# A hybrid GLA and dilated-attention layer on eight cores: x loaded as bf16 through the GpSimd DMA queue, and the transposes of the GLA output moved to the merge

## The reference, cut to what matters

```python
h = x @ w_in
gq, gk, gv, gg, g_lr, dq, dk, dv, gate_a, gate_b = jnp.split(h, SPLIT_AT, axis=-1)
logd = jax.nn.log_sigmoid((g_lr @ w_gk_b + b_gk).astype(jnp.float32)) / GLA_NORMALIZER
o, S = gla_recurrence(...)
o = o * lax.rsqrt(jnp.mean(jnp.square(o), -1, keepdims=True) + NORM_EPS) * gla_norm
o = o * jax.nn.silu(gg.reshape(B, T, GLA_HEADS, GLA_DV).astype(jnp.float32))
ya = o.reshape(B, T, GLA_V).astype(x.dtype) @ w_br_gla
...
m = jax.nn.sigmoid(gate_a) * ya + jax.nn.sigmoid(gate_b) * yb
x = layer_norm(ALPHA * x + m @ w_out, ln1_g, ln1_b)
```

## Time and profile before

| | us |
|---|---|
| median of 2 runs | 5650.87 (5649.4 to 5652.34) |
| the profiled execution, its own time | 5676.41 |
| span of that execution, slowest core | 5675.1 |
| spans of the 8 cores | 5634.0 to 5675.1 |
| mean granted clock of PE, share of full speed | 0.738 to 0.743 |

### The profile page before, as it was taken

How to read it: one execution, slowest core, us unless ns; L and a number is a source line. 1 busy time by engine, 2 the same in 40 slices (tenths; PEclk the granted TensorE clock), 3 DMA queues, 4 the chain that set the end, 5 groups by cost and what they waited for, 6 DMA issues and landing times.

```text
span 5675.1 us, 71363 instructions; the slowest of 8 cores (5634.0 to 5675.1 us)
## 1 busy us (share of the span) xinstructions
PE 3560.3 (63%) x23137; PEld 2106.4 (37%) x23326; DVE 2144.8 (38%) x4185; ACT 1498.2 (26%) x3227; POOL 561.9 (10%) x666
## 2 busy tenths in 40 slices
PE   0346777778658658658658658658658656344454
PEld 0123334335335435335435335435435424233333
DVE  1111223344444444435435435435435434322223
ACT  0112222224224224224224224224224213111111
POOL 0000111110100100100100100100100111100011
PEclk9667788886876876876876876876876877755556
DMA  9998444442532532532532532532532555576774
GB/s 130 147 151 164 132 139 146 153 147 72 170 110 73 180 114 72 177 111 80 175 113 80 171 117 80 170 118 83 174 114 87 165 179 180 188 154 134 141 173 151
DMA packets 219423, 768.24 MB, mean 135 GB/s; under 512 B 19788, under 2 KB 41102, under 8 KB 216600
## 3 DMA queue, kind: packets, MB, share of 16 engines
q0 software_dynamic: 166176, 650.26, 43.1%
q1 hardware_dynamic: 52888, 113.41, 6.1%
HBM read 832.46 MB, written 75.91 MB: 160 GB/s over the span
## 4 chain that ended last, share of the span: by engine, by line
PE 52%; DVE 17%; DMA 13%; issue 7%; ACT 7%; another core or an unknown queue 2%; DVEq 1%; ACTq 0%; SPq 0%; POOLq 0%
PE pr L230 42%; DMA sb_wb<-scr_w_in 6%; PE pl L230 5%; PE pr L234 3%; DVE sb_g_xres L252 2%; PE pb L234 2%; DVE sb_g_cacc L261 1%; DVE sb_Sst L261 1%; DVE sb_stats L692 1%; DMA sb_g_xres<-xh 1%; ACT sb_aext L241 1%; ACT sb_kTc L241 1%; DVE sb_rA L252 1%; DMA sb_wb<-scr_w_out 1%
## 5 line engine op out<-in xcount | busy, mean ns | idle before, releaser
L230 PE MATMUL pr<-sb_wb,sb_g_xT 128*128 128x512 bf16 x4028 | 1099.3, 430 | 158.2 <-DMA sb_wb<-scr_w_in 133.4
L230 PE MATMUL pr<-sb_g_xT,sb_wb 128*128 128x256 bf16 (+3 forms) x4008 | 493.2, 282 | 400.9 <-DMA sb_wb<-scr_w_in 168.4
L230 PEld LDWEIGHTS pr<-sb_wb,sb_g_xT 128*128 128x128 bf16 x4184 | 451.4, 110 | 755.5 <-issue 410.6
L139 POOL DMA_DIRECT2D sb_wb<-scr_w_in x318 | 281.7, 887 | 2960.1 <-PE pr L230 2828.6
L230 PEld LDWEIGHTS pr<-sb_g_xT,sb_wb 128*128 128x128 bf16 (+1 forms) x4008 | 381.3, 102 | 509.6 <-issue 453.1
L249 ACT ACTIVATE sb_PT<-pr 128x512 bf16<-128x512 f32 x816 | 483.1, 597 | 214.7 <-PE pr L230 207.0
L234 PE MATMUL pr<-sb_idf,sb_g_xres 128*128 128x128 f32 x784 | 152.4, 357 | 590.4 <-DVE sb_g_xres L252 253.7
L230 PE MATMUL pr<-sb_g_qT,sb_kTr 64*128 64x128 bf16 x3264 | 464.9, 295 | 0.0
L234 PEld LDWEIGHTS pr<-sb_idf,sb_g_xres 128*128 128x128 f32 x784 | 122.8, 186 | 617.8 <-issue 616.9
L230 PE MATMUL pl<-sb_Vr,sb_PT 128*128 128x65 bf16 x3264 | 321.5, 239 | 36.5 <-DVE sb_PT L252 28.4
L230 PEld LDWEIGHTS pr<-sb_g_qT,sb_kTr 64*128 64x128 bf16 x3264 | 263.9, 124 | 73.2 <-issue 2.8
(11 more groups left out here) (229 smaller groups left out, 4434.8 us busy)
## 6 DMA issues: line engine op xcount, KB each, us to landing
sb_wb<-scr_w_in POOLq DMA_DIRECT2D x284, 1024.0 KB, 7.3
sb_wb<-scr_w_up POOLq DMA_DIRECT2D x100, 1024.0 KB, 8.2
sb_wb<-scr_w_down POOLq DMA_DIRECT2D x40, 1024.0 KB, 8.1
sb_g_xres<-xh SPq DMA_DIRECT2D x64, 512.0 KB, 5.7
sb_kvc<-kvc POOLq DMA_DIRECT2D x16, 2048.0 KB, 13.0
sb_lnp<-lnp SPq DMA_DIRECT2D x60, 512.0 KB, 4.0
sb_wb<-scr_w_brg POOLq DMA_DIRECT2D x20, 1024.0 KB, 7.5
sb_wb<-scr_w_out POOLq DMA_DIRECT2D x20, 1024.0 KB, 8.1
```

The lines of the kernel that those rows point to most:

```text
L139: ins = q.h.dma_start(out=out, in_=in_, **kw)
L230: fw.op(pe, lambda: nc.tensor.matmul(out, lhsT, rhs, start=start, stop=stop), reads=reads, writes=writes, skip_self=True)
```

## The change

It has two parts and a small one.

1. **x as bf16, loaded by POOL.** A new buffer `xbf` (two tiles, bf16) is filled by `issue_xb` through POOL's queue, which converts on the way. The first group's load is issued before the loop; the load for the next group is issued right after the transposes of the present one and ahead of the weight loads of `gla_prep`. The transposes read `xbf` by `transpose_b16`: eight blocks into the one bank `pb` and one copy of 1024 columns per tile, instead of two buffers and two copies of 512. The float32 load of x by SP is kept only in full groups, for the residual.
2. **The transposes of the GLA output later.** `onb` becomes a buffer per tile of the group (`onb[:, j, ...]`), and the transposes leave `gla_out_norm` for a function of their own, `gla_out_T(j)`, which `merge_out` calls for all tiles before its first projection.
3. `cvo`, the staging tile of the convolution state, becomes a name for `rA`. The `K_PAD` lines do nothing unless a variable is set.

```diff
-        onb = T("onb", (128, 1024), BF16)
...
-        cvo = T("cvo", (32, 512))
+        cvo = rA
...
+        xbf = Tp("xbf", (128, G, D), BF16)
...
-                stt(onb[:, h * 256:(h + 1) * 256], PL[h // 2][:, (h % 2) * 256:(h % 2 + 1) * 256], ssq[:, 4 + h:5 + h],
+                stt(onb[:, j, h * 256:(h + 1) * 256], PL[h // 2][:, (h % 2) * 256:(h % 2 + 1) * 256], ssq[:, 4 + h:5 + h],
...
-            transpose_b16(lambda c: onb[:, c * 128:(c + 1) * 128], 8,
-                          lambda c0, n_: onT[:, c0:c0 + n_, j * 128:(j + 1) * 128], [R("onb")], [R("onT", j)])
+
+        def gla_out_T(j):
+            transpose_b16(lambda c: onb[:, j, c * 128:(c + 1) * 128], 8,
+                          lambda c0, n_: onT[:, c0:c0 + n_, j * 128:(j + 1) * 128], [R("onb", j)], [R("onT", j)])
...
         def merge_out(tiles):
             n = len(tiles)
             ln_load(0)
+            for j in range(n):
+                gla_out_T(j)
...
-        _issued = False
+
+        def issue_xb(tiles_):
+            for j_, t_ in enumerate(tiles_):
+                fw.dma(pool, xbf[:, j_, :], xsrc(t_), writes=[R("xbf", j_)])
+
+        issue_xb(_glist[0][0])
...
-            load_x(tiles, xsrc, ridx if kind != "state" else None, issued=_issued)
-            _issued = False
-            if kind != "full" and _gi + 1 < len(_glist):
-                _nt, _nk = _glist[_gi + 1]
-                issue_x(_nt, xsrc, ridx if _nk != "state" else None)
-                _issued = True
+            if kind == "full":
+                for j, t in enumerate(tiles):
+                    fw.dma(sp, xres[:, j, :], xsrc(t), writes=[R("xres", j)])
+            if kind != "state":
+                for j, t in enumerate(tiles):
+                    fw.dma(sp, ropet[j][:], rope_d[ridx(t)], writes=[R("ropet", j)])
+            for j, t in enumerate(tiles):
+                transpose_b16(lambda c, j=j: xbf[:, j, c * 128:(c + 1) * 128], 8,
+                              lambda c0, n_, j=j: xT[:, c0:c0 + n_, j * 128:(j + 1) * 128], [R("xbf", j)], [R("xT", j)])
+            if _gi + 1 < len(_glist):
+                issue_xb(_glist[_gi + 1][0])
```

More of the change, by code:

```diff
@@ L345, in alloc_group_bufs @@
             d["ggn"] = TT("ggn", (128, g_, 1024), BF16)
-            d["onT"] = TT("onT", (128, 8, n_), BF16)
+            d["onT"] = TT("onT", (128, 8, n_), BF16); d["onb"] = TT("onb", (128, g_, 1024), BF16)
             d["qT"] = [TT(f"qT{g}", (128, g_, 4, 128), BF16) for g in range(3)]
@@ L356, in _build @@
         Ebl = _gb["Ebl"]; eblT = _gb["eblT"]; qtT = _gb["qtT"]; ktT = _gb["ktT"]; khat = _gb["khat"]; vb = _gb["vb"]
-        ggn = _gb["ggn"]; onT = _gb["onT"]; qT = _gb["qT"]; attnT = _gb["attnT"]; mb = _gb["mb"]; mT = _gb["mT"]
+        ggn = _gb["ggn"]; onT = _gb["onT"]; onb = _gb["onb"]; qT = _gb["qT"]; attnT = _gb["attnT"]; mb = _gb["mb"]; mT = _gb["mT"]
         cacc = _gb["cacc"]; gl = _gb["gl"]; yT = _gb["yT"]; pT = _gb["pT"]
@@ L361, in _build @@
         Sst = Tp("Sst", (128, NH, DV)); Sbf = Tp("Sbf", (128, NH, DV), BF16)
+        xbf = Tp("xbf", (128, G, D), BF16)
         aext = [Tp(f"aext{i}", (128, 2 + NMAX)) for i in range(2)]
         tails = Tp("tails", (128, NFC, 2))
+        _pad = int(os.environ.get("K_PAD", "0"))
+        if _pad:
+            padbuf = Tp("padbuf", (128, _pad))
         RS = [NDEL[g] + G - 1 for g in range(3)]
@@ L882, in _build @@
                 tp(ps[0:2, c * 128:(c + 1) * 128], tails[:, fc, :], idf[:], [R("tails"), RC], [rp])
-            evac(cvo[0:2, 0:nf * 128], ps[0:2, 0:nf * 128], [rp], [R("cvo")], eng=dve)
-            fw.dma(sp, cv_p[:, f4 * 512:f4 * 512 + nf * 128], cvo[0:2, 0:nf * 128], reads=[R("cvo")])
+            evac(cvo[0:2, 0:nf * 128], ps[0:2, 0:nf * 128], [rp], [R("rA")], eng=dve)
+            fw.dma(sp, cv_p[:, f4 * 512:f4 * 512 + nf * 128], cvo[0:2, 0:nf * 128], reads=[R("rA")])
         ck(9)
@@ L1052, in _build @@
                     tp(ps[0:32, c * 128:(c + 1) * 128], cvs[:, fc, :, :].rearrange("p b j -> p (b j)"), idf[:], [R("cvs"), RC], [rp])
-                evac(cvo[0:32, 0:nf * 128], ps[0:32, 0:nf * 128], [rp], [R("cvo")], eng=dve)
-                fw.dma(sp, cv_s[:, f4 * 512:f4 * 512 + nf * 128], cvo[0:32, 0:nf * 128], reads=[R("cvo")])
+                evac(cvo[0:32, 0:nf * 128], ps[0:32, 0:nf * 128], [rp], [R("rA")], eng=dve)
+                fw.dma(sp, cv_s[:, f4 * 512:f4 * 512 + nf * 128], cvo[0:32, 0:nf * 128], reads=[R("rA")])
             ple(tiles, lambda t: ps_d, lambda t: y_s)
```

2 lines of the change are left out of this document (1 added, 1 removed).

## The result

The changed kernel took 5796.35 us (median of 11 runs, 5768.43 to 5944.03) beside 5672.67 us for the kernel before on the same chip (10 runs). The ratio is 1.0199, 95% interval 1.0169 to 1.0229: 112 us more on 5651, between 96 and 129. The forecast was 109 more. The ratios of the experiments further down are, in the same way, to the kernel before on the same chip. The profiled execution took 5768.43 us with a span of 5767.0 us; the spans of its cores are 5735.3 to 5767.0, on the mean 94.0 us longer than those of before.

What follows compares the result with a forecast made beforehand. PE was taken as the bound, with 52% of the chain of waits. Start 11, state seams 65, kv seams 69, full seams -19 and moved transposes -17 sum to +109 us on 5651: 5760, range 5695 to 5815.

Steps and rivals of the forecast that it cites:

- The gate: In POOL's queue, next x loads wait for PE's transposes and hold the weight loads behind them; price 8.5 us.
- T to V0: From the end of x's last transposes to the group's first value projection: 8.5 us, between 6.5 and 13.4.
- Start: At the kernel's start, the second pair of conversions must follow the first transposes: +11 us, between 0 and 30.
- State seams: Between state groups: 7.4 us lost in each of 8, 59; two more cost about 6 together; sum 65.
- the clock: PE's lower granted clock behind a wait for weights: 0.6 us per state seam, 1.8 per kv, 1.3 per full.
- Kv seams: Between kv groups and into the first full group, 8 in all: 8.6 us lost each, 69 us.
- Full groups: At seams between full groups: 1.4 us gained in each of 7, 9 in the last; sum -19.
- The moved transposes: GLA output transposes moved to the merge: net gain 1.9 us in 8 groups, 2.2 in the last; -17.
- A: Rival at the seams: the gate costs nothing, loads land before PE can use them; -78 us, 5573; chance 0.07.
- B: Rival in the full groups: the wait for onb is given back whole, 139 us instead of 17; 5638; chance 0.10.
- C: Rival at the seams: all weight loads trail, first value projection 3.5 us later; +80 us, 5840; chance 0.15.
- Its small form: Full seams alone: each of two x issues waits for a layer norm operation, 2.6 us in each of 7; +18, 5778.

Runs made afterwards that it cites:

- e3: The kernel before plus one tiny POOL load ahead of each group's weight loads, held until PE has transposed the group's x: ratio 1.0302.
- e1: The changed kernel with the next group's x loads issued behind the present group's weight loads instead of ahead: ratio 0.988 to the kernel before.
- e4: The changed kernel with only tile 0 of the next x ahead of the weight loads and tile 1 behind them: ratio 0.997 to the kernel before.
- e2: The kernel before with only the later transposes of the GLA output (onb) added, x loaded and transposed as before: ratio 0.9959.
- e5: The changed kernel with x loads behind the weight loads and onb again transposed inside the output norm: ratio 0.988 to the kernel before.

## Why the prediction was right, point by point

**The gate** is shown three ways: it costs the 3% alone (e3), taking it away turns the sign (e1), and releasing it at an earlier transpose takes away the part that this release time decides (e4). The predicted time of 5760 was 109 above 5651; the runs give 112, the core means 94.0. The mechanism was right, but that 109 and 112 lie so close is in part luck. By the core means the start came out 8 us below my terms, the rest of the state stage 6 below, the part behind the last V0 6 below, and in the kv seams two errors cancelled.

**T to V0** I had put at 8.5 us from single rows. It is 9.1 in state seams, 10.3 in kv seams and 12.3 in full seams. With no x ahead of the weights (e3) it is 8.7, 9.5 and 8.9. So the sum of issue, landing and handing over was nearly right. (The lower end of 6.5 that I gave does not follow from the 2.8 beside it, which makes 5.2.) The bytes of x were undersized: I had 0.3 us, and the difference between the two lines of the table, of which e3 has only 1 KB in place of x, is 0.4, 0.8 and, beside `y_p` and the float32 x, 3.4 (forecast 1.8 there). By the formula of the Trainium skill, page "DMA: Bandwidth & Descriptors", section "Anatomy of one DMA — SWDGE (gpsimd) path", 1 MB lands in 4.4 us, an estimate by that page. The trace does not agree: in the kv seam above, V0's load was issued at 932.30 + 0.88 = 933.18 and its first reader ran at 941.15, 8.0 us later, and in e3 6.2 us later (937.88 to 944.10).

**Start.** Predicted 11, and 7.4 for the seam of group 7, which lies in this stage: 18.4. Measured 10.4. On the mean over the cores that seam went from 11.5 to 16.7, 5.2 us, so that some 5 us are left for the conversions, although the second pair was issued 19 us later. On the same mean the last conversion lands at 537.0 us, before at 531.0. The term of 11 was about twice too large, as far as can be told where e2 shows 5.2 with no change at all. The gap in the queue was there: from 90 to 110 us the DMA share was 0.41 where the kernel before had 0.98, which is 11 us of it. But from 150 us until all was converted it was 1.00 (to 548 us) where it had been 0.98 (to 545 us), and 0.02 of 395 us is 8 us, a rough figure, since the shares are rounded. So the gap was partly made up.

**State seams.** Predicted 58 for the rest of the stage, measured 51.4. Six seams between two-tile groups cost 7.0 each (predicted 7.4). What I had overlooked is the seam into the last state group with two tiles: only one tile of x is to be fetched for the group behind it, POOL is released by the first transposes, and the seam cost 1.0 instead of 7.4. The two light ones cost 3.3 and 6.4, where I had 6 for both. The 0.6 for the clock was already in the 7.4, and nothing of it shows inside the groups: from V0 to the end of a state group it is 23.2 us before and 23.1 after.

**Kv seams.** Predicted 69, measured 72.3: 8 seams at 8.5, and 0.5 a group within. Here two errors met. T to V0 was 1.8 longer, and the clock cost 0.5 where I had 1.8. The row I took it from is right for the stretch: the 32 matmuls of the value projection that began at 941.15 took 9.60 us in all, against 7.07 in the earlier trace rows. But in many groups the kernel before ran the small matmuls behind it more slowly than the changed one (first fence before, second fence changed, the same place of a kv group):

```profile
960.24 1.71 PE L230 MATMUL pr<-sb_useg,sb_g_spb 128*128 128x1 f32 x8
```

```profile
954.29 0.95 PE L230 MATMUL pr<-sb_useg,sb_g_spb 128*128 128x1 f32 x8
```

The means over the 8 kv groups of all cores say the same: the value projection takes 7.2 us before and 9.2 after, at a mean granted clock of 0.98 and 0.76; from its end to the end of the group it is 35.6 and 34.1 us, at 0.82 and 0.86. What is lost at the seam is mostly given back behind it. Why the clock is higher there, no run shows.

**Full groups.** Predicted -34 up to V0 of the last group, measured -31.8. Six seams were 0.3 longer and not 1.4 shorter, since T to V0 was 12.3 and not 10.0; the copies behind the layer norm came where I had put them, T at 16.4 (predicted 16.75). The seventh was 6.6 shorter by the same one-tile case that I had overlooked, the eighth 10.1 (predicted 9). What lies between the seams was 17.2 shorter over 8 groups (predicted 15).

**The moved transposes.** The terms were of the right size in sum, but not in their parts. I had 5.6 gained and 3.7 lost at the merge; in e2, from the same points, 7.6 were gained, 3.2 lost in the projections behind, and 3.5 at the merge, and 0.9 more were gained behind the merge, which I cannot assign. The loss in the projections was not in my sum. In the last group I had 2.2, and it is 5.6 in e2. Added to e1 they bring 8 us by the core means, nearly all in the last group, and nothing that the ratio can tell.

**Rivals.** A described a kernel whose T to V0 is 3.1 us; e1 is that kernel, and its ratio of 0.988 gives 5583 us where A had 5573. A's parts were not right: its 0.5 for a kv seam does not follow from my own terms (2.65 + 3.1 - 4.4 = 1.35), and in e1 a kv seam is 1.2 longer than before and the group behind it another 1.2, 18.9 in all where A had 4; the full groups made up for it. B is refuted by e2. C is not what happened: V0 comes 0.6 and 1.8 us later than I took in state and kv seams, and 2.3 later than the 10.0 I had in full seams, not 3.5. Its small form, each x issue held by a layer norm operation, does not show. In the full seam above POOL issues x at 2179.41 in 0.55 us while DVE's 2.55 us operation, begun at 2177.81, is running, 0.57 after the transposes end. I had drawn on the Trainium skill, page "SBUF — State Buffer", section "SBUF: two separate sides", for it, and had applied it wrongly: what that section says of DVE holding off GpSimd's descriptor writing is for operations in a two-port mode. For an operation with two inputs from SBUF, as this one is, it names a conflict with a GpSimd operation that reads SBUF. So the trace neither bears that rule out nor speaks against it.

**Behind the last V0** the core means are 8.3 us shorter (94.0 in all, 102.3 up to there); I had 2.2. The experiments place it with the moved transposes. In the seven kernels of the table that have them this part is 6.4 to 9.3 us shorter than before, and in the two that do not, e3 and e5, it is 1.9 and 2.7 longer. Most of it is the last group, from its V0 to the decoding part: 301.8 us before, 295.1 to 297.3 with the moved transposes, 303.8 and 306.2 without.

## What to carry to other kernels

A load that waits for a consumer gates everything behind it in an in-order queue: put a prefetch behind the loads that have no such wait, and after any reordering look once more at what each load waits for and what stands behind it. Here the position of one load decided between 1.0199 and 0.988, and between 1.0142 and 0.9733. And before a wait is removed, read what its engine waits for next: the waits for `onb` (147 us) were worth 23 (between 9 and 38).

## What the runs showed of the hardware

- A wait of PE costs twice: at the same place of a full group, 24 projections of 512 columns took 5.34 us without and 7.61 us behind a wait of 5.42 (e5 and e1). But the other way too: the granted clock behind the value projection of a kv group rose from 0.82 to 0.86 when the projection itself fell from 0.98 to 0.76, so that a seam 8.5 us longer cost only 0.5 more within its group. Here the clock price read off one stretch was too high.
- In the state groups of the changed kernel four weight loads are issued back to back through POOL, the small `C_LR` block and three of 1 MB. The three landed with a median of 10.1 us from their issue, where 1 MB loads issued one at a time had 5.9 in the kernel before. A gate does not only delay loads, it bunches them.
